# Attention, routing and last stage of a decoder layer: earlier loads of w_out and modulation rows, a smaller first load, and a gated sum on TensorE

## The chip, the cores and the metric

One core of one Trainium2 chip runs the whole program. The metric is device time in microseconds (us), as the median of several runs. The profiler records one execution. Engines are called as in the profile: PE is TensorE (PEld its weight loads), DVE is VectorE, ACT is ScalarE, POOL is GpSimd, SP is SyncE.

## The reference, cut to what matters

A prompt of 2048 tokens and a group of 8 samples with 4 new tokens each (positions from 4096 on, with paged K and V) go through one layer with the same weights, everything in float32:

```python
mod = (silu(c) @ w_ada + b_ada)                      # shift1, scale1, gate1, shift2, scale2, gate2: one row per sequence
proj = (rms_norm(x, norm_mix) * (1 + scale1) + shift1) @ w_in          # q | k | v | xr | yb
# stick-breaking attention, 8 heads of 64:
z = q k^T / 8 + bias;  A[t,s] = sigmoid(z[t,s]) * prod_{s<j<t} (1 - sigmoid(z[t,j]))  for s < t
attn = rms_norm(A v, norm_attn);  rg = rms_norm(rg_lru(conv(xr)) * gelu(yb), norm_rg)
x = x + gate1 * (concat(attn, rg) @ w_out)                              # w_out is 1024 x 1024
xn2 = rms_norm(x, norm_ffn) * (1 + scale2) + shift2
# 32 experts: best group of 4, two best experts e0, e1 in it, with gates g0, g1
ffn = g0 * expert[e0](xn2) + g1 * expert[e1](xn2)
y = rms_norm(x + gate2 * ffn, final_norm)
```

The samples' attention reads 32 pages of 128 keys each, for K and for V, named by a page table: 256 pages of 256 KB each of K and of V.

## The kernel before

The program is a row of phases. Each is a block in which every engine runs its own written-out list of instructions; semaphores order them, and a barrier stands between blocks. There is no planner: the order is that of the Python loops.

**Attention (`attention_phase`, L813).** The prompt's attention goes over 4 pairs of heads and 16 query tiles of 128; 80 items (pair, two query tiles, chunk of 512 keys) of four steps each make 320 steps ("ticks", loop L1348 for PE, L1067 for ACT, L1184 for DVE). In each, PE multiplies q and k (L1244), ACT takes two sigmoids (L1090, L1092), DVE scans (L1208) and multiplies (L1114), PE transposes (L1257) and multiplies by v (L1277). Between them lie 16 units of 19 ticks for the samples. Unit u takes K pages 4 x 4 at a time: `k_turn` (L1290) transposes them out of two buffers `kp` (4 pages each), `sample_scores` (L1300) multiplies them with q, one unit later `sample_values` (L1317) multiplies by the V pages in two buffers `vp`. Each goes with `g = 4 * u + j`.

SP issues in this order (L948 to L973): the page table; `load(0)`, which is q, k and v of the first pair (`qT`, `kT`, `vv`, 1 MB each, L931 to L935); eight small loads of gain and bias (L952, L953), for which DVE waits once at tick 1 (L1211); then for each u and j: wait until group g - 2 has been transposed, four K pages (L921). After group 1 come the new v rows, `load(1)` of the second pair and a wait for the zeros; after j = 1 and j = 3 of each unit `zero_rows` (L937), which writes 1 MB of zeros to the buffers of routing in HBM. `load(2)` and `load(3)` follow units 4 and 8. POOL issues the V pages (L1011), each when its buffer is free. The transposed K lies in `kTs`, which is the memory of `rowsP` and `rowsS`. q, k of the pairs lie in the memory of the first expert's weights.

**Routing (`router_phase`, L1374).** 17 tiles of tokens (the 32 sample tokens first, then 16 of 128). For each tile PE multiplies by the two halves of `w_out` (L1580), DVE multiplies by the modulation row gate1 and adds x (L1645, L1650), then come norm, transposes, logits, the choice of experts and POOL's scatters. At its head SP issues nf_row, the first half of `w_out`, the first rg tile, the second half, x and the router's weights and biases (L1439 to L1461), and POOL the modulation rows `rowsS` and `rowsP` (L1476, L1477). DVE waits for `small` (nf_row and the two biases) and `rows` before its first work (L1720, L1721); PE waits for each half of `w_out` (L1572).

**Experts (`experts_phase`, L1792)** is untouched.

**Last stage (`final_phase`, L1987).** 17 tiles again, with four buffers of two rows per token. POOL gathers the two experts' rows of each token by indirect DMA (L2038); ACT scales the first by its gate (L2048); DVE adds the second times its gate (L2071) and, for even tiles, multiplies by gate2 (L2077); for odd tiles POOL does this (L2029). DVE adds x (L2085). ACT squares, sums and roots (L2053, L2055); DVE takes the reciprocal (L2090) and scales by `final_norm` (L2094); SP stores (L2019). POOL waits for tile i - 3 to be added before it gathers tile i + 1.

## Time and profile before

| | |
|---|---|
| median of 3 runs | 3034.0 us (3031.31 to 3037.3) |
| profiled execution, its own time | 3027.28 us |
| its span, first to last instruction | 3025.3 us |
| attention, about | 728 to 1572 us of the span |
| routing, about | 1573 to 1883 us |
| experts, about | 1884 to 2908 us |
| last stage, about | 2917 us to the end |

Busy time is time in which an engine had an instruction; idle time is put down to what ended it ("<-"). The granted clock is PE's, as a share of 2.4 GHz. A matmul of 512 float32 columns stands as two records that overlap.

### The profile page before, as it was taken

What the parts mean: (1) busy time and instruction counts of PE and PEld (TensorE: products, weight loads), DVE (VectorE), ACT (ScalarE), POOL (GpSimd) and SP (SyncE); (2) the same over time, 40 slices, a digit from 0 to 9 for tenths busy, and PEclk for the clock granted to TensorE, in tenths of its full rate; (3) what the DMA queues carried; (4) which work ended last, traced back from release to release, by engine and by line L of the source; (5) the groups of instructions that cost most, each with busy time, mean ns of one, the idle gap of its engine ahead of it and who ended that gap; (6) DMA issues with size and microseconds to landing.
All of it is one profiled execution on the core that took longest, in us unless ns stands there. A gap on an engine that the chain in (4) does not pass through costs nothing. (4 is left out here: it accounts for less than half of the span.)

```text
span 3025.3 us, 45306 instructions
## 1 busy us (share of the span) xinstructions
PE 2673.0 (88%) x15001; PEld 1337.1 (44%) x15001; DVE 1362.8 (45%) x2735; ACT 973.7 (32%) x1841; POOL 504.4 (17%) x679
## 2 busy tenths in 40 slices
PE   7999999986899898999969999499999998999940
PEld 3444444432444444444434555255555554455520
DVE  2232314132687787887866777222122221122237
ACT  2222222212677676777751212111001010001024
POOL 0101010101011111112110222211111111111136
PEclk9999999997899999999999999699999999999975
DMA  8020201028566667667645433676986579868737
GB/s 313 14 84 14 84 14 56 14 83 322 172 234 232 232 225 239 218 214 252 203 158 162 140 126 132 217 247 213 308 279 210 196 240 362 289 230 278 243 118 248
DMA packets 275673, 575.74 MB, mean 190 GB/s; under 512 B 59278, under 2 KB 75727, under 8 KB 271236
## 3 DMA queue, kind: packets, MB, share of 16 engines
q1 hardware_dynamic: 192464, 425.37, 40.5%
q0 software_dynamic: 82704, 148.06, 15.5%
q8 instruction: 89, 1.46, 0.2%
q14 instruction: 92, 0.75, 0.1%
q10 hardware_dynamic: 324, 0.10, 0.0%
HBM read 460.86 MB, written 112.29 MB: 189 GB/s over the span
## 5 line engine op out<-in xcount | busy, mean ns | idle before, releaser
L1921 PE MATMUL h<-w,xT 128*64 128x256 f32 x5120 | 588.4, 383 | 21.7 <-DMA w<-in_w 17.2
L1921 PEld LDWEIGHTS h<-w,xT 128*64 128x64 f32 x5120 | 362.6, 138 | 242.9 <-issue 73.5
L1208 DVE TENSOR_TENSOR_SCAN left<-leave,left 128x512 f32<-128x512 f32 (+3 forms) x320 | 358.6, 1121 | 162.9 <-ACT leave L1090 161.7
L418 PE MATMUL bank<-xnT,w_in 128*128 128x512 f32 x768 | 330.3, 592 | 0.0
L1934 PE MATMUL yb<-w,hT 128*64 128x512 f32 x1280 | 307.0, 600 | 0.0
L1902 ACT ACTIVATE sg<-h 128x128 f32<-128x128 f32 x160 | 44.4, 278 | 688.5 <-PE h L1921 688.5
L1011 POOL DMA_DIRECT2D vp<-in_cache_v x256 | 137.8, 538 | 690.1 <-issue 685.1
L1580 PE MATMUL pb<-w_out,featT 128*128 128x512 f32 x512 | 227.7, 597 | 1.0 <-DVE t L1645 1.0
L418 PEld LDWEIGHTS bank<-xnT,w_in 128*128 128x128 f32 x768 | 145.6, 190 | 181.8 <-issue 180.3
L1967 DVE TENSOR_TENSOR sg<-sg,h 128x128 f32<-128x128 f32 x160 | 46.1, 288 | 387.5 <-ACT sg L1902 387.5
L418 PE MATMUL bank<-w_in,xnT 128*128 128x512 f32 x512 | 220.4, 592 | 0.0
L1090 ACT ACTIVATE leave<-zb,nbiasP 128x512 f32<-128x512 f32 (+3 forms) x320 | 203.8, 637 | 8.6 <-PE zb L1250 8.6
L1092 ACT ACTIVATE take<-zb,biasP 128x512 f32<-128x512 f32 (+3 forms) x320 | 206.4, 645 | 0.0
L1257 PE MATMUL tb<-ident,take 128*128 128x128 f32 x1088 | 187.7, 289 | 20.6 <-DVE take L1114 16.0
L1114 DVE TENSOR_TENSOR take<-take,left 128x512 f32<-128x512 f32 (+3 forms) x320 | 194.8, 609 | 15.8 <-DVE left L1208 0.4
L1244 PE MATMUL zb<-w 64*128 64x512 f32 (+3 forms) x640 | 166.1, 597 | 31.3 <-ACT take L1092 19.1
L1257 PEld LDWEIGHTS tb<-ident,take 128*128 128x128 f32 x1088 | 116.7, 142 | 165.7 <-issue 106.2
L1290 PE MATMUL tb<-ident,kp 128*128 128x128 f32 x1024 | 160.3, 280 | 30.3 <-DMA kp<-in_cache_k 16.8
L1277 PE MATMUL ob<-wT,vv 128*64 128x256 f32 (+1 forms) x1152 | 183.4, 398 | 1.7 <-ACT wT L1022 1.6
L1022 ACT ACTIVATE wT<-tb 128x512 f32<-128x512 f32 (+3 forms) x240 | 131.0, 546 | 100.7 <-PE tb L1257 99.9
L1876 POOL DMA_DIRECT2D ys_d<-y x82 | 69.2, 844 | 509.1 <-DMA ys_d<-y 443.8
L418 PEld LDWEIGHTS bank<-w_in,xnT 128*128 128x128 f32 x512 | 97.3, 190 | 122.5 <-issue 122.5
(373 smaller groups left out, 2841.6 us busy)
## 6 DMA issues: line engine op xcount, KB each, us to landing
w<-in_w SPq DMA_DIRECT2D x96, 2048.0 KB, 23.5
vp<-in_cache_v POOLq DMA_DIRECT2D x256, 256.0 KB
kp<-in_cache_k SPq DMA_DIRECT2D x256, 256.0 KB
ys_d<-zeros SPq DMA_DIRECT2D x32, 816.0 KB
slab<-in_w_ada SPq DMA_DIRECT2D x24, 1024.0 KB, 13.4
ys_d<-y POOLq DMA_DIRECT2D x83, 256.0 KB, 9.9
x_in<-xs_d POOLq DMA_DIRECT2D x162, 128.0 KB, 6.3
w_in<-in_w_in SPq DMA_DIRECT2D x5, 2048.0 KB, 20.6
```

Source lines behind the costliest of these rows:

```text
L418: mm = pe.matmul(ps[:, :], w, m, start=(i == 0), stop=(i == len(parts) - 1))
L1090: act.activation(leave[n % 4][:, 0:cols], zb[n % 3][:, 0:cols], ACT.Sigmoid, scale=-SCALE, bias=keep["nbiasP"][:, head:head + 1]).then_inc ...
L1092: act.activation(take[n % 4][:, 0:cols], zb[n % 3][:, 0:cols], ACT.Sigmoid, scale=SCALE, bias=keep["biasP"][:, head:head + 1]).then_inc(s_ ...
L1114: dve.tensor_tensor(take[n % 4][:, 0:cols], take[n % 4][:, 0:cols], left[n % 4][:, 1:cols + 1], ALU.mult).then_inc(s_w, 1)
L1208: dve.tensor_tensor_scan(left[n % 4][:, 0:cols][:, ::-1], leave[n % 4][:, 0:cols][:, ::-1], leave[n % 4][:, 0:cols][:, ::-1], left[n % 4][ ...
L1244: mm = pe.matmul(zb[(n + par) % 3][:, 0:cols], qT[pair % 2][half, t * P:t * P + P], kT[pair % 2][half, c * GRP:c * GRP + cols], start=True ...
L1257: mm = pe.transpose(to[:, j * P:j * P + P], take[n % 4][:, j * P:j * P + P], ident[:, :])
L1277: mm = pe.matmul(o[64 * par:64 * par + 64, q0:2 * P], vv[pair % 2][:, c * TPG + j, 64 * par:64 * par + 64], wT[m % 2][par][:, j, :, :].rea ...
L1290: mm = pe.transpose(to[:, i * P:i * P + P], kp[g % 2][:, i, f * P:f * P + P], ident[:, :])
L1580: mm = pe.matmul(pb[half][0:n, :], lhs, w_out[:, c, half * 512:half * 512 + 512], start=(c == 0), stop=(c == KC - 1))
L1921: mm = pe.matmul(h[half][q * G:q * G + G, 0:2 * P], xT[:, c % (XW // P), c // (XW // P) * G:c // (XW // P) * G + G], w13[i][:, c, :, cols] ...
L1934: mm = pe.matmul(yb[p * G:p * G + G, :], hT[:, half, q * G:q * G + G], w2[i][:, q * (EC // STRIPS) + half, p * XW:p * XW + XW], start=(hal ...
```

## The change

- **Attention, start.** The first 512 columns of q and k of pair 0 are loaded first with a semaphore of their own, before the page table; the rest follows. PE waits for the first at item 0 and for the rest at item 2. `load(1)` moves from after group 1 to after unit 1. The zero rows of unit 0's j = 1 go, and each later one moves back by one place; the last stands behind all K pages.
- **Attention, end.** `kp` and `vp` now lie in the memory of `w_out`, which is kept over attention and routing, in the layout (half, chunk, 512). SP loads the first half of `w_out` when the last K group is transposed, then both modulation rows when the last sample scores are done, and the second half when the last sample values are done. The loads of the same name leave the head of routing, from SP and from POOL.
- **Last stage.** Six gather buffers instead of four. ACT makes two diagonal matrices of the gates per tile out of the identity; PE multiplies them with the two gathered row sets and sums them in PSUM (four sets of two banks). DVE multiplies the sum by gate2 (reading PSUM) for every tile. POOL only gathers.

```diff
@@ attention_phase
-        kp = [k.sb(f"kp{i}", [P, PPC, WA]) for i in range(2)]
-        vp = [k.sb(f"vp{i}", [P, 4, WA]) for i in range(2)]
+        kp = [keep["w_out"][:, 0, PPC * i:PPC * i + PPC, :] for i in range(2)]
+        vp = [keep["w_out"][:, 1, PPC * i:PPC * i + PPC, :] for i in range(2)]
...
-                def load(pair):
+                def load(pair, start=0):
...
-                    sp.dma_start(qT[i], io["qT_d"][rows, :]).then_inc(s_kq[i], 16)
-                    sp.dma_start(kT[i], io["kT_d"][rows, :]).then_inc(s_kq[i], 16)
+                    sp.dma_start(qT[i][:, start:], io["qT_d"][rows, start:]).then_inc(s_kq[i], 16)
+                    sp.dma_start(kT[i][:, start:], io["kT_d"][rows, start:]).then_inc(s_kq[i], 16)
...
+                sp.dma_start(qT[0][:, 0:GRP], io["qT_d"][0:P, 0:GRP]).then_inc(s_kq0, 16)
+                sp.dma_start(kT[0][:, 0:GRP], io["kT_d"][0:P, 0:GRP]).then_inc(s_kq0, 16)
                 sp.dma_start(pages[:, :], io["page_table"].rearrange("(a b) n -> a (b n)", a=1)).then_inc(s_pg, 16)
-                load(0)
+                load(0, GRP)
...
                         if g == 1:
                             new_rows(0)
-                            load(1)
                             sp.wait_ge(s_set, 1)
-                        if j == 1:
+                        if j == 1 and u:
+                            zero_rows(2 * u - 1)
+                        if j == 3:
                             zero_rows(2 * u)
-                        if j == 3:
-                            zero_rows(2 * u + 1)
+                            if u == 1:
+                                load(1)
                             if u == 2:
                                 new_rows(1)
                             if u in (4, 8):
                                 load(u // 4 + 1)
+                zero_rows(2 * NU - 1)
+                w_out_d = io["w_out"][0].rearrange("(c p) n -> p c n", p=P)
+                turned(sp, "k_turn", NU - 1, 4 * FC - 1)
+                sp.dma_start(keep["w_out"][:, 0, :, :], w_out_d[:, :, 0:512]).then_inc(sems["w_out0"], 16)
+                turned(sp, "scores", NU - 1)
+                sp.dma_start(keep["rowsS"][:, :, :], io["mod_d"][1:, :]...).then_inc(sems["rows"], 16)
+                sp.dma_start(keep["rowsP"][:, :, :], io["mod_d"][0:1, :]...).then_inc(sems["rows"], 16)
+                sp.wait_ge(s_spv, PPC * NU)
+                sp.dma_start(keep["w_out"][:, 1, :, :], w_out_d[:, :, 512:1024]).then_inc(sems["w_out1"], 16)
                 sp.wait_ge(s_fill, 48 * NE)
...
-                    if m % PPI == 0 and tile == 0:
+                    if m == 0 and tile == 0:
+                        pe.wait_ge(s_kq0, 32)
+                    elif (m == 2 if pair == 0 else m % PPI == 0) and tile == 0:
                         pe.wait_ge(s_kq[pair % 2], 32 * (pair // 2) + 32)
@@ router_phase
-        w_out = k.sb("w_out", [P, KC, D])
+        w_out = keep["w_out"]
...
-                sp.dma_start(w_out[:, :, 0:512], w_out_d[:, :, 0:512]).then_inc(s["w0"], 16)
...
-                sp.dma_start(w_out[:, :, 512:1024], w_out_d[:, :, 512:1024]).then_inc(s["w1"], 16)
...
-                pool.dma_start(keep["rowsS"][:, :, :], io["mod_d"][1:, :]...).then_inc(s["rows"], 16)
-                pool.dma_start(keep["rowsP"][:, :, :], io["mod_d"][0:1, :]...).then_inc(s["rows"], 16)
...
-                        pe.wait_ge(s[f"w{half}"], 16)
+                        pe.wait_ge(sems[f"w_out{half}"], 16)
...
-                        mm = pe.matmul(pb[half][0:n, :], lhs, w_out[:, c, half * 512:half * 512 + 512], ...)
+                        mm = pe.matmul(pb[half][0:n, :], lhs, w_out[:, half, c, :], ...)
@@ final_phase, POOL
                 for i in range(NTL):
-                    n = size[i]
-                    if i >= SETS:
-                        gated(i - SETS)
-                    if i >= SETS:
-                        pool.wait_ge(s["x2"], i - SETS + 1)
+                    n, b = size[i], i % YS
+                    if i >= YS:
+                        pool.wait_ge(s["mm"], i - YS + 1)
...
@@ final_phase, ACT (first)
-                    act.wait_ge(s_y[b], 32 * (i // SETS) + 32)
-                    act.activation(yy[b][0:n, 0, :], yy[b][0:n, 0, :], ACT.Copy, scale=gates[0:n, 0, i:i + 1]).then_inc(s["g0"], 1)
+                    if i >= SETS:
+                        act.wait_ge(s["mm"], i - SETS + 1)
+                    for j in range(2):
+                        last = act.activation(diag[b][0:n, j, 0:n], keep["ident"][0:n, 0:n], ACT.Copy, scale=gates[0:n, j, i:i + 1])
+                    last.then_inc(s["dg"], 1)
...
@@ final_phase, PE (new)
+                for i in range(NTL):
+                    n, b = size[i], i % SETS
+                    pe.wait_ge(s["dg"], i + 1)
+                    pe.wait_ge(s_y[i % YS], 32 * (i // YS) + 32)
+                    if i >= SETS:
+                        pe.wait_ge(s["x2"], i - SETS + 1)
+                    for half in range(2):
+                        cols = slice(512 * half, 512 * half + 512)
+                        for j in range(2):
+                            mm = pe.matmul(both[b][0:n, cols], diag[b][0:n, j, 0:n], yy[i % YS][0:n, j, cols], start=(j == 0), stop=(j == 1))
+                    mm.then_inc(s["mm"], 1)
@@ final_phase, DVE (summed and added in one)
+                    dve.wait_ge(s["mm"], i + 1)
+                    if i >= SETS:
+                        dve.wait_ge(s_st[b], 16 * (i // SETS))
+                    dve.tensor_tensor(out[b][0:n, :], both[b][0:n, :], rows[n][0:n, 3, :], ALU.mult)
+                    dve.drain()
                     dve.wait_ge(sems["x1_s" if i == 0 else ...], 16)
+                    dve.tensor_tensor(x1[i][0:n, :], x1[i][0:n, :], out[b][0:n, :], ALU.add).then_inc(s["x2"], 1)
...
                 summed(0)
-                added(0)
-                summed(1)
                 for i in range(NTL):
-                    if i + 2 < NTL:
-                        summed(i + 2)
                     if i + 1 < NTL:
-                        added(i + 1)
+                        summed(i + 1)
                     normed(i)
```

## Rows read from the trace of the kernel before

**Rows 1.** Part 1 of the page: busy us, share of the span, instructions.

```profile
PE 2673.0 (88%) x15001; PEld 1337.1 (44%) x15001; DVE 1362.8 (45%) x2735; ACT 973.7 (32%) x1841; POOL 504.4 (17%) x679
```

**Rows 2.** Timeline at the start of attention: start, us, engine, line, work [idle before].

```profile
735.64 0.80 PE L1244 MATMUL zb<-w 64*128 64x128 f32 x4 [11.51 <-DMA w<-kT_d]
...
745.30 0.15 DVE L1213 TENSOR_SCALAR s_nbias<-s_bias 128x1 f32<-128x1 f32 x1 [6.92 <-DMA s_bias<-in_sb_bias]
...
751.83 8.71 SPq L939 DMA_DIRECT2D xs_d<-zeros  x2
...
754.78 0.60 PE L1290 MATMUL tb<-ident,kp 128*128 128x128 f32 x4
...
763.30 11.38 SPq L921 DMA_DIRECT2D kp<-in_cache_k  x8
...
773.54 1.11 PE L1290 MATMUL tb<-ident,kp 128*128 128x128 f32 x4 [8.72 <-DMA kp<-in_cache_k]
```

**Rows 3.** Windows there: busy by engine, granted clock, DMA share, GB/s.

```profile
772.00:782.00 10.00, 8.29 (x42) 4.62 (x44) 4.04 (x6) 5.30 (x11) 0.00 (x0) 0.69 0.62 194
```

**Rows 4.** Timeline of PE: the first sample_scores matmul of units 4, 5, 8, 9, 15.

```profile
988.80 0.62 PE L1300 MATMUL tb<-rowsP,q_blk 128*32 128x512 f32 x2
...
1042.65 0.62 PE L1300 MATMUL tb<-rowsP,q_blk 128*32 128x512 f32 x2
...
1187.65 1.04 PE L1300 MATMUL tb<-rowsP,q_blk 128*32 128x512 f32 x2 [1.58 <-ACT wT L1022]
...
1242.76 0.62 PE L1300 MATMUL tb<-rowsP,q_blk 128*32 128x512 f32 x2
...
1528.71 0.62 PE L1300 MATMUL tb<-rowsP,q_blk 128*32 128x512 f32 x2
```

**Rows 5.** Timeline of the end of attention and the head of routing.

```profile
1565.31 1.06 PE L1317 MATMUL s_ob<-vp,s_wT 128*32 128x512 f32 x8
...
1572.69 0.63 ACT L1517 ACTIVATE o_sq<-oT 128x512 f32<-128x512 f32 x1 [2.13 <-PEq L92]
...
1589.28 9.34 PE L1580 MATMUL pb<-w_out,xnT_s 128*32 128x512 f32 x16 [18.07 <-DMA w_out<-in_w_out]
...
1599.60 7.05 PE L1580 MATMUL pb<-w_out,xnT_s 128*32 128x512 f32 x16
...
1599.97 1.21 DVE L1723 SCALAR_TENSOR_TENSOR rowsS<-rowsS,nf_row 32x1024 f32<-32x1024 f32 x1 [11.23 <-DMA b_r<-in_b_router]
...
1607.70 7.11 PE L1580 MATMUL pb<-w_out,featT 128*128 128x512 f32 x16 [1.05 <-DVE t L1645]
```

**Rows 6.** Windows there.

```profile
1530.00:1540.00 10.00, 8.46 (x58) 2.95 (x50) 5.55 (x9) 6.87 (x12) 0.00 (x0) 1.00 0.00 1
1570.00:1580.00 10.00, 0.30 (x1) 0.11 (x1) 0.88 (x4) 1.20 (x3) 2.09 (x13) 0.67 0.61 212
```

**Rows 7.** Timeline of the last stage: its first ACT, two POOL products ten tiles apart, its last DVE.

```profile
2922.89 1.15 ACT L2048 ACTIVATE w<-w,gates 32x1024 f32<-32x1024 f32 x1 [19.44 <-DMA w<-ys_d,ydest_u]
...
2945.55 2.61 POOL L2029 TENSOR_TENSOR w<-w,rowsP 128x1024 f32<-128x1024 f32 x1
...
3001.30 2.61 POOL L2029 TENSOR_TENSOR w<-w,rowsP 128x1024 f32<-128x1024 f32 x1
...
3020.47 1.28 DVE L2094 SCALAR_TENSOR_TENSOR w<-w,ssq,f_row 128x1024 f32<-128x1024 f32 x1
```

**Rows 8.** The tile view of the last stage: ns min/median/max, first and last start.

```profile
L2038 POOL DMA_INDIRECT w<-ys_d,ydest_u x34: 897/1132/2042, 2918.7 to 3000.3; - x34
L2071 DVE SCALAR_TENSOR_TENSOR w<-w,gates x17: 1267/1278/3650, 2924.2 to 3012.1; 128x1024 f32<-128x1024 f32 x16, 32x1024 f32<-32x1024 f32 x1
L2085 DVE TENSOR_TENSOR w<-w,w x17: 1204/1220/1226, 2926.8 to 3017.4; 128x1024 f32<-128x1024 f32 x16, 32x1024 f32<-32x1024 f32 x1
L2053 ACT ACTIVATE junk<-w x17: 1039/1057/1058, 2931.9 to 3018.7; 128x1024 bf16<-128x1024 f32 x16, 32x1024 bf16<-32x1024 f32 x1
L2094 DVE SCALAR_TENSOR_TENSOR w<-w,ssq,f_row x17: 1274/1285/3139, 2938.4 to 3020.5; 128x1024 f32<-128x1024 f32 x16, 32x1024 f32<-32x1024 f32 x1
```

**Rows 9.** The last stage in windows, and what the DMA view of 2916 to 3025 moved.

```profile
2940.00:3004.00 64.00, 0.00 (x0) 0.00 (x0) 49.35 (x52) 27.57 (x44) 50.65 (x30) 0.50 0.82 275
...
DMA packets 7202, 26.10 MB, mean 239 GB/s; under 512 B 832, under 2 KB 832, under 8 KB 7200
```

More of the change, by code:

```diff
@@ L810, in _, with attention_phase @@
                 dve.drain()
-def attention_phase(nc, io, keep):
+def attention_phase(nc, io, keep, sems):
     PAIRS, TPAIRS, PPI = H // 2, NT // 2, 20
@@ L885, in attention_phase @@
             k.sem(f"p4_{n}") for n in ("set", "z", "lv", "tk", "in", "sc", "w", "t", "cd", "ca", "pv", "o", "fill"))
-        s_kq = [k.sem(f"p4_kq{i}") for i in range(2)]
+        s_kq0, s_kq = k.sem("p4_kq_first"), [k.sem(f"p4_kq{i}") for i in range(2)]
         s_v = [k.sem(f"p4_v{i}") for i in range(2)]
@@ L1418, in router_phase @@
         s = {n: k.sem(f"p6_{n}") for n in (
-            "w0", "w1", "wr", "small", "rows", "set", "cons",
+            "wr", "small", "set", "cons",
             "oh", "or", "oT", "fe", "hd", "mm0", "mm1", "ev0", "ev1", "x1", "xs", "xn", "xT", "xe",
@@ L1429, in router_phase @@
         x_src = io["x_prompt"][0].rearrange("(t p) n -> t p n", p=P)
-        w_out_d = io["w_out"][0].rearrange("(c p) n -> p c n", p=P)
         size = [NS] + [P] * NT
@@ L1579, in out_product @@
                             lhs = keep["rgT_new"][:, c - FC, :]
-                        mm = pe.matmul(pb[half][0:n, :], lhs, w_out[:, c, half * 512:half * 512 + 512], start=(c == 0), stop=(c == KC - 1))
+                        mm = pe.matmul(pb[half][0:n, :], lhs, w_out[:, half, c, :], start=(c == 0), stop=(c == KC - 1))
                     mm.then_inc(s[f"mm{half}"], 1)
@@ L1720, in _ @@
                 dve.wait_ge(s["small"], 48)
-                dve.wait_ge(s["rows"], 32)
+                dve.wait_ge(sems["rows"], 32)
                 for n in (NS, P):
@@ L2062, in _ @@
                     squared(i)
+            @block.tensor
+            def _(pe):
+                for i in range(NTL):
[9 more added lines that the diff above has]
+                    mm.then_inc(s["mm"], 1)
             @block.vector
@@ L2140, in build_program @@
         with ExitStack() as inner:
-            keep["oT"] = Kit(nc, inner, clears=False).sb("oT", [P, FC, SEQ])
-            attention_phase(nc, io, keep)
-            router_phase(nc, io, keep)
+            ki = Kit(nc, inner, clears=False)
+            keep["oT"], keep["w_out"] = ki.sb("oT", [P, FC, SEQ]), ki.sb("w_out", [P, 2, KC, 512])
+            for name in ("w_out0", "w_out1", "rows"):
+                sems[name] = k.sem(name)
+            attention_phase(nc, io, keep, sems)
+            router_phase(nc, io, keep, sems)
         with ExitStack() as inner:
```

44 lines of the change are left out of this document (12 added, 32 removed).

## The prediction, made before the change was run

> **What bounds the kernel now.** Part 1 of the page comes first: PE is busy 88% of the span [rows 1]. That is an average, so I went by stage, with windows, and then read the timeline wherever PE was idle. Only three places of the change touch time in which PE does nothing useful. At the start of attention PE sits idle 8.72 us for K pages, and then works at the lower clock [rows 2, 3]. At the head of routing it sits idle 18.07 us for w_out [rows 5]. In the last stage it does nothing at all and its clock stands at 0.50, while DVE, ACT and POOL hand each tile round [rows 7 to 9]. Between these places the order of the work is unchanged, and an earlier start there is an earlier end.
>
> **Part 1, start of attention.** PE's first matmul waits until 735.64 for k [rows 2]. With 256 KB of q and of k in front instead of 1 MB each, it would start some 4 us sooner (a quarter of the data, and the span begins this phase at about 728). I give this nothing: at tick 1 DVE waits for the bias until 745.30, after 6.92 us idle [rows 2], and that load stands behind the same 3 MB of q, k and v as before. Two more issues stand ahead of it, and SP's are a few tenths each, so I charge 0.4 us. Bounds: 1 us lost to 4 gained.
>
> What helps is load(1) and the first zero rows leaving their place. SP was held 8.71 us in the issue of the zeros (behind 3 MB of load(1)), and so issued the K pages of group 2 at 763.30, though the group 0 that frees their buffer was transposed at 755.4 [rows 2]. Now these pages go out at about 757 (some 1.7 us behind the release, as 763.30 stands behind the 761.5 at which SP had finished), four in 3 to 4 us, and land by about 764. PE asked for them at 764.8 (773.54 less 8.72). So the 8.72 us go, with at most 1 or 2 left. The clock goes with them: from 772 to 782 it was granted at 0.69, which is half speed for 6.2 of the 10 us, so PE, which restarted at 773.54, ran some 4.7 us at half speed and lost 2.3 [rows 3]. Together 11.0 us, bounds 6 and 12.
>
> load(1) comes back after unit 1, at j = 3, where load(2) and load(3) stand in units 4 and 8, ahead of the next unit's pages. What such a load costs can be read directly: from unit 4's scores to unit 5's it is 53.85 us, from 8's to 9's 55.11, and from 9's to 15's 285.95 / 6 = 47.66 [rows 4]. The extra is 6.2 and 7.4; I take 6.8. Bounds 4 and 9. The other zero rows keep one per two groups, so they are worth nothing; the last two stand together behind the last pages, and the DMA engines then lie idle (share 0.00 at 1530 to 1540 [rows 6]).
>
> Sum of part 1: -0.4 + 11.0 - 6.8 = +3.8 us gained. Bounds: 7 lost, 9 gained.
>
> **Part 2, end of attention and head of routing.** The first half of w_out (2 MB) and the rows (2.5 MB) go out at about 1526 and 1532, into DMA engines that are idle, 40 us ahead of need: they cost nothing. If that cover were missing they would delay the last V pages. The second half goes out when the last sample values end, at 1566.4 [rows 5], and at the 275 / 0.82 = 335 GB/s that full DMA engines give [rows 9] lands after 6.3 us and some latency, at about 1575. Its first user is PE's second product, not before 1580. SP's last wait, for the zeros, is long met, so the block still ends with DVE.
>
> Routing starts at 1572.7 [rows 5]. Before, PE began its products at 1589.28 and reached the next tile's at 1607.70, 18.4 us later, of which 1.05 were a wait for DVE. It now begins at 1572.8, so this tile is reached at 1572.8 + 17.4 = 1590.2; if the clock is still high, 2.3 us earlier (the first eight products took 9.34 us against 7.05 at full clock). The clock: 0.67 over 1570 to 1580 is full speed until about 1573.4 [rows 6], just after the new start, so it may hold. DVE is the other leg: it starts at 1599.97, when the router's bias lands, and frees PE at 1607.70, 7.7 us later. That bias was issued at the end of SP's queue, behind 4 MB of w_out, and POOL's 2.5 MB shared the engines. Left ahead of it are the rest of the second half, 0.5 MB of nf_row, 0.25 MB of rg, 0.13 MB of x and the router's weights, in many small pieces. 0.9 MB at 335 GB/s is 2.7 us behind 1575, and the small pieces I put at 4 us: about 1581.5, bounds 1579.5 and 1588. DVE then frees PE at 1589.2. I take 1590: gain 1607.7 - 1590 = 17.7 us. Bounds 11.5 (bias at 1588) and 20. The rest of routing runs PE nearly full, so the gain stays.
>
> **Part 3, last stage.** Before, 10 tiles took 3001.30 - 2945.55 = 55.75 us, 5.58 each [rows 7]; the chain is POOL's gathers, its 2.61 us product, DVE's add, and POOL again, since four buffers tie the gather to the add. The product leaves POOL and the buffers are six, so this loop is cut. What is late next, per tile:
> - DVE: two tensor_tensor and one scaling, whose starts lie 1.2 us or so apart (1220 and 1285 ns each [rows 8]), and a reciprocal: 3.95 us. A product that reads PSUM I price as the nearest, 1.22.
> - PE: four products of 512 columns. Eight took 7.05 us at full clock [rows 5], so 3.5; at half clock twice that, 6.9.
> - POOL: two gathers, 1132 ns in the median and up to 2042 [rows 8], with 0.3 between: 2.9, at most 4.7.
> - ACT: two small copies, square, root: about 2.3 by a square of 1.06 [rows 8].
> - DMA: 26.10 MB at 335 GB/s is 78 us for the stage [rows 9], 4.6 a tile.
>
> DVE's account: PE starts tile 0 at 2922.9 [rows 7], at the low clock, 6 us; then 17 x 3.95 = 67.2 us, to 2996.1; the last DVE work ended at 3021.8, 3.5 us before the span's end, so 2999.6: 25.7 gained. DMA's account: from about 2921, 78 less 3 for the last two stores, the last gather lands at 2996; then PE 3.5, DVE 2.5, ACT 1.6, DVE 1.4 and 3.5: 3008.5, 17 gained. They are close enough to disturb each other; I take 21. Bounds 8 and 28.
>
> The shared port is weighed here. A DVE scaling took 3650 ns instead of 1278 where POOL's product ran beside it, and gathers took 0.90 to 2.04 us, the long ones beside DVE work [rows 8]. The Trainium skill, SBUF — State Buffer (Who interferes with whom), says that a DVE instruction with two SBUF inputs contends with a GpSimd instruction that reads SBUF, not with one that only writes it. By it the gathers would be spared, POOL would need 34 x 1.24 = 42 us and be off the path; by the row's long ones it is the first rival below.
>
> **Sum.** 3.8 + 17.7 + 21 = 42.5 us. Against the profiled execution's own 3027.28 us that is 2984.8. The median of the runs shown is 6.7 us above it; I predict for such a median: 3034.0 - 42.5 = 2991.5, rounded 2991.
>
> **Rivals.**
> 1. Gathers become the bound. For it: every second pair took 2.0 us each [rows 8]. Against it: the other pairs took about 1. At 2.3 us for all 34 the last is issued at 2918.7 + 78 = 2997, lands 7 us later, and 12.5 us of tail give 3016.5: 9 gained instead of 21. Time 3003.
> 2. The early K wait stays while load(1) costs its 6.8, because pages wait for something else than SP. For it: V pages and v of pair 0 share the engines. Against it: SP's own hold of 8.71 us. Time 2991 + 11 = 3002.
> 3. The bias lands late (1588): 6 us less, 2997; together with 2, 3008.
> 4. The other side: PE's clock stays low in the last stage. Place: each tile's four products, 6.9 us, and up to 7.6 with an exposed weight load before each. 17 x 7.6 = 129 us from 2922.9, and 9.2 of tail: 3061.3, 36 lost there. Against the 21.5 gained elsewhere that is 14.5 slower: time 3048. It decides from 6.8 us a tile on. For it: PE was at 0.50 throughout [rows 9] and will wait for gathers. Against it: a PE busy without a break was always granted the full clock within some us (the first products of routing rose within their 9.34 us [rows 5]). The Trainium skill, TensorE: Matmul & The Clock Gate (HAM oscillation — how this bites in real kernels), describes it: loops that wait for DMA between bursts of matmuls fall back to the low clock and start each burst slow.
>
> **How the numbers follow.** Forecast (36 to 50 us gained) 0.70; rival 1 0.12; rival 2 or 3 0.13; rival 4 0.03; 0.02 for a mishap that eats the gain. Measurement of this kernel can tell about 0.2%, 6 us, from no change. Faster 0.94, same 0.02, slower 0.04. The range reaches to rivals 1 to 3 and, below, to all upper bounds but a few us: 2976 to 3006.
>
> **What would show it.** In the changed kernel's timeline: no K wait near 765, and a new one of 5 to 7 us some 10 us after the last of unit 1's scores; the first bias wait of DVE still near 745; routing's first product at its block's start and the second tile 17 to 18 us after; DVE in the last stage near 4 to 4.6 us a tile, PE at 1.00 after the first tiles, POOL waiting. The forecast is wrong if gathers keep POOL busy without a break, if PE's clock stays at 0.50, or if routing waits for anything beyond 1585.

## The result and the profile after

| | before | after |
|---|---|---|
| median (lowest to highest) | 3032.65 us (3030.08 to 3037.3) | 2993.23 us (2989.49 to 2995.77) |
| profiled execution: own time, span | 3027.28, 3025.3 us | 2991.91, 2990.2 us |

The ratio is 0.9867, with a 95% interval of 0.985 to 0.9884: 39.4 us less between the medians. The forecast of 2991 us lies 2.2 us below the median and inside the spread of the runs. What follows reads the three places of the prediction again.

Part 1 of the page after, against [rows 1]: PE is busy 66 us more, by the products of the last stage, and POOL and DVE a little less.

```profile
PE 2739.4 (92%) x15137; PEld 1363.8 (46%) x15137; DVE 1347.6 (45%) x2726; ACT 963.5 (32%) x1858; POOL 471.7 (16%) x669
```

**Start of attention.** The timeline after, against [rows 2] (start, duration, engine, line, work, idle time before it and what ended it):

```profile
731.56 6.45 SPq L954 DMA_DIRECT2D s_gain<-in_norm_attn  x1
...
736.02 0.80 PE L1258 MATMUL zb<-w 64*128 64x128 f32 x4 [10.83 <-DMA w<-kT_d]
...
744.46 8.08 SPq L921 DMA_DIRECT2D w_out<-in_cache_k  x8
...
747.51 0.15 DVE L1225 TENSOR_SCALAR s_nbias<-s_bias 128x1 f32<-128x1 f32 x1 [8.76 <-DMA s_bias<-in_sb_bias]
...
751.38 1.12 PE L1304 MATMUL tb<-ident,w_out 128*128 128x128 f32 x4 [2.50 <-DMA w_out<-in_cache_k]
...
759.18 3.64 SPq L921 DMA_DIRECT2D w_out<-in_cache_k  x4
...
849.24 0.98 PE L1304 MATMUL tb<-ident,w_out 128*128 128x128 f32 x4 [4.34 <-DMA w_out<-in_cache_k]
...
998.86 1.12 PE L1304 MATMUL tb<-ident,w_out 128*128 128x128 f32 x4 [9.46 <-DMA w_out<-in_cache_k]
```

The K pages of group 2 go out at 759.18 and the 8.72 us are gone; from 772 to 782 the granted clock is 1.00, not 0.69 [rows 3]. But the bias lands at 747.51, 2.2 us later than before, and PE's first product comes no sooner in spite of its smaller loads. The moved load costs a new wait of 4.34 us at 849.24.

```profile
772.00:782.00 10.00, 9.05 (x66) 5.56 (x67) 8.97 (x17) 8.99 (x19) 0.00 (x0) 1.00 0.61 193
```

The first sample_scores products of units 4, 5 and 15, against [rows 4]. Unit 4 is 5.1 us earlier than before; of this only 0.3 is left at unit 15, since the waits behind load(2) and load(3), which the change does not move, are longer in this profile (9.46 instead of 6.36 us behind load(2)).

```profile
983.71 0.62 PE L1314 MATMUL tb<-rowsP,q_blk 128*32 128x512 f32 x2
...
1039.83 0.62 PE L1314 MATMUL tb<-rowsP,q_blk 128*32 128x512 f32 x2
...
1528.37 0.62 PE L1314 MATMUL tb<-rowsP,q_blk 128*32 128x512 f32 x2
```

**Head of routing**, against [rows 5, 6]. The first product starts with its block; DVE is released at 1583.62, since SP is held 4.74 us in the issue of the first router bias; the second tile's product comes 16.35 us earlier than before.

```profile
1566.10 0.40 SPq L984 DMA_DIRECT2D w_out<-in_w_out  x1
...
1572.38 8.72 PE L1589 MATMUL pb<-w_out,xnT_s 128*32 128x512 f32 x16 [1.52 <-PEq L92]
...
1574.82 4.74 SPq L1467 DMA_DIRECT2D b_r<-in_b_group  x1
...
1583.62 1.21 DVE L1732 SCALAR_TENSOR_TENSOR rowsS<-rowsS,nf_row 32x1024 f32<-32x1024 f32 x1 [8.65 <-DMA b_r<-in_b_router]
...
1591.35 1.10 PE L1589 MATMUL pb<-w_out,featT 128*128 128x512 f32 x2 [2.20 <-DVE t L1654]
```

```profile
1570.00:1580.00 10.00, 7.92 (x15) 1.95 (x16) 1.41 (x7) 0.85 (x2) 1.50 (x14) 0.83 0.90 234
```

**Last stage.** From the issue of f_row to the end of the span it took 107.4 us and takes 85.9. Its timeline and its tile view, against [rows 7, 8]:

```profile
2904.31 0.36 SPq L2023 DMA_DIRECT2D f_row<-in_final_norm  x1
...
2909.59 25.87 PE L2079 MATMUL both<-w,diag 32*32 32x512 f32 x46 [18.69 <-DMA w<-ys_d,ydest_u]
...
2916.71 1.21 DVE L2091 TENSOR_TENSOR w<-both,rowsS 32x1024 f32<-32x1024 f32 x1 [24.86 <-PE both L2079]
...
2922.63 1.23 DVE L2091 TENSOR_TENSOR w<-both,rowsP 128x1024 f32<-128x1024 f32 x1 [3.42 <-PE both L2079]
...
2985.37 1.28 DVE L2101 SCALAR_TENSOR_TENSOR w<-w,ssq,f_row 128x1024 f32<-128x1024 f32 x1
```

```profile
L2079 PE MATMUL both<-w,diag x136: 592/592/1222, 2909.6 to 2977.2; 128*128 128x512 f32 x128, 32*32 32x512 f32 x8
L2041 POOL DMA_INDIRECT w<-ys_d,ydest_u x34: 883/945/1926, 2905.1 to 2956.2; - x34
...
L2091 DVE TENSOR_TENSOR w<-both,rowsP x16: 1203/1218/1225, 2922.6 to 2981.0; 128x1024 f32<-128x1024 f32 x16
```

In windows (busy us of PE, PEld, DVE, ACT, POOL, then granted clock, DMA share, GB/s), against [rows 9]: PE runs its first tiles at 0.50 and rises between 2920 and 2924. From then on DVE is busy 3.6 to 3.85 of 4 us. The DMA engines move 410 to 422 GB/s from 2920 to 2928 and again from 2940 to 2964, which I had not thought they could; between the two it is 340.

```profile
2916.00:2920.00 4.00, 4.00 (x5) 1.51 (x5) 2.42 (x2) 0.76 (x1) 3.08 (x4) 0.50 1.00 395
2920.00:2924.00 4.00, 4.00 (x9) 1.81 (x8) 1.23 (x1) 2.55 (x6) 2.86 (x4) 0.84 1.02 413
2924.00:2928.00 4.00, 4.00 (x10) 1.71 (x9) 3.58 (x4) 2.03 (x5) 2.44 (x2) 1.00 1.02 410
2944.00:2948.00 4.00, 3.82 (x9) 1.44 (x8) 3.85 (x5) 2.03 (x5) 2.29 (x3) 1.00 1.03 422
```

### The profile page after: what moved, and what is told of

Read it like the earlier page. It is cut to its first block and busy times, and to the rows that moved or that the text cites. A ratio compares the mean times of both kernels' runs of the same rounds, so it can differ in the third digit from the quotient of the medians.

```text
span 2990.2 us, 45603 instructions
## 1 busy us (share of the span) xinstructions
PE 2739.4 (92%) x15137; PEld 1363.8 (46%) x15137; DVE 1347.6 (45%) x2726; ACT 963.5 (32%) x1858; POOL 471.7 (16%) x669
## 5 line engine op out<-in xcount | busy, mean ns | idle before, releaser
L1023 POOL DMA_DIRECT2D w_out<-in_cache_v x256 | 137.4, 537 | 689.2 <-issue 687.6
L1258 PE MATMUL zb<-w 64*128 64x512 f32 (+3 forms) x640 | 164.4, 591 | 30.3 <-ACT take L1104 18.7
L1304 PE MATMUL tb<-ident,w_out 128*128 128x128 f32 x1024 | 159.9, 280 | 31.7 <-DMA w_out<-in_cache_k 23.2
```

The source lines that it names most:

```text
L1258: mm = pe.matmul(zb[(n + par) % 3][:, 0:cols], qT[pair % 2][half, t * P:t * P + P], kT[pair % 2][half, c * GRP:c * GRP + cols], start=True ...
L1304: mm = pe.transpose(to[:, i * P:i * P + P], kp[g % 2][:, i, f * P:f * P + P], ident[:, :])
```

## The experiments

All start from the changed kernel. The table reads each profile by stage, in us. The first four columns count from SP's first issue in attention: the end of DVE's bias wait, the first transposed K page, the first product with the samples' q in unit 0, and the first sample_scores product of unit 15. "To tile 2" is from there to the second routing tile's product. "Experts" is from DVE's first fill of `y` there (1916.75 us before) to the issue of f_row, and "last" from that issue to the end of the span. The ratio is to the kernel before, run beside it.

| kernel | bias | first K | unit 0 | unit 15 | to tile 2 | experts | last | median, ratio (95%) |
|---|---|---|---|---|---|---|---|---|
| before | 17.5 | 20.6 | 64.5 | 800.9 | 79.0 | 1001.2 | 107.4 | 3032.7 |
| after | 18.6 | 22.5 | 55.4 | 799.5 | 63.0 | 1003.8 | 85.9 | 2993.2, 0.9867 (0.985 to 0.9884) |
| e10, after again | 18.7 | 22.5 | 55.4 | 795.7 | 63.1 | 1012.1 | 85.4 | 2993.2, 0.9863 (0.9844 to 0.9882) |
| e1, old last stage | 18.7 | 22.6 | 55.3 | 794.7 | 63.0 | 1012.1 | 106.8 | 3013.8, 0.9922 (0.9904 to 0.9939) |
| e2, load(1) early | 18.7 | 22.4 | 65.0 | 801.0 | 63.2 | 1010.3 | 86.9 | 3000.6, 0.9893 (0.9875 to 0.991) |
| e3, whole first loads | 17.5 | 20.7 | 53.1 | 792.9 | 63.1 | 1002.3 | 85.5 | 2988.7, 0.9849 (0.9833 to 0.9866) |
| e4, w_out loaded late | 18.7 | 22.7 | 55.2 | 796.7 | 80.1 | 1003.2 | 85.6 | 3010.2, 0.9921 (0.9898 to 0.9944) |
| e5, four buffers | 18.6 | 22.5 | 55.1 | 791.8 | 63.2 | 1003.7 | 86.6 | 2987.3, 0.9845 (0.9814 to 0.9877) |
| e6, bias by ACT | 11.7 | 22.8 | 55.9 | 797.6 | 62.8 | 1013.9 | 85.9 | 2997.0, 0.9867 (0.9835 to 0.99) |
| e7, loads in parts | 18.6 | 22.6 | 55.5 | 786.3 | 62.7 | 1010.0 | 86.4 | 2983.1, 0.982 (0.9787 to 0.9852) |
| e8, warm PE; bias first | 18.6 | 22.6 | 55.4 | 793.4 | 60.7 | 1009.0 | 83.3 | 2986.0, 0.984 (0.9803 to 0.9877) |
| e11, start order | 10.0 | 12.8 | 44.4 | 782.2 | 62.6 | 1012.5 | 85.5 | 2979.8, 0.9824 (0.9804 to 0.9845) |
| e12, all | 10.5 | 13.4 | 45.6 | 774.8 | 60.7 | 1009.1 | 85.8 | 2970.4, 0.9793 (0.9777 to 0.9808) |

Two columns give the noise. The experts' code is the same in all rows and takes 1001 to 1014 us; the waits for x_in behind it differ from run to run of one kernel (41.8 us in 9 waits after, 48.8 in 13 in e10). And six kernels (after, e10, e1, e4, e5, e8) have the same attention up to unit 15, and reach it at 791.8 to 799.5 us, mean 795.3. The kernel before gave medians of 3033 to 3036 us beside the experiments. But e5's median lies 5.9 us below that of the changed kernel, though its last stage is no shorter. So medians tell some 6 us and more, and the stages must be read for anything smaller.

The spread at unit 15 has a place. From one unit's first sample_scores product to the next, the six agree within 0.3 us up to unit 1 (107.8 to 108.1 us after SP's first issue), and most of what they differ by lies in the three stretches behind a load: unit 1 to 2 (49.7 to 51.4 us), 4 to 5 (53.1 to 56.1) and 8 to 9 (54.4 to 56.1). So an edit at the start is read best at unit 1 or 2. Before, these were at 118.4 and 165.1 us; in the six, unit 2 is at 157.5 to 159.4, mean 158.6.

**e1: the last stage as it was** (all of `final_phase`).

```diff
-                            mm = pe.matmul(both[b][0:n, cols], diag[b][0:n, j, 0:n], yy[i % YS][0:n, j, cols], start=(j == 0), stop=(j == 1))
+                    act.activation(yy[b][0:n, 0, :], yy[b][0:n, 0, :], ACT.Copy, scale=gates[0:n, 0, i:i + 1]).then_inc(s["g0"], 1)
...
```

> The changed kernel with the last stage as it was (GpSimd and VectorE do the gated sum, four gather buffers); everything else as changed. Theory: the stage's 21.5 us (107.4 before, 85.9 after, from the issue of f_row to the end of the span) come from its own work, whatever lies ahead of it: 2993.2 + 21.5 = 3014.7 us, and the stage is again 107 to 108 us long. Rival: part of the 21.5 is a gift of what was changed ahead (the stage begins with other queues and another clock): the stage stays under 102 us and the time under 3009 us.

The stage is 106.8 us again, 20.9 more than after and 21.4 more than in e10; the median is 20.6 us higher. Its gain is its own.

**e2: load(1) and the zero rows at their old places.**

```diff
                             new_rows(0)
+                            load(1)
...
-                            if u == 1:
-                                load(1)
```

> The changed kernel with load(1) and the zero rows back at their old places (load(1) in unit 0 behind the second K page, zero rows at j of 1 and 3); small first loads kept. Theory: the K page stall returns in unit 0 (8.7 us, with some low clock behind it), and the 4.6 us that unit 1 to 2 pays for load(1) go; the later loads cost 3.3 us more after the change than before it, and if that hangs on the order of the zero rows they go too. In sum within 2 us of the changed kernel if the later loads' cost goes (2993 to 2995 us), 4 to 6 us slower if it stays (2997 to 2999 us). Rival: what left unit 0 (8 us and 2.2 of the bias wait) is all gain and unit 1 would have paid its 4.6 us anyway: 8 to 10 us slower, 3001 to 3003 us.

The stall is back, behind the same hold of SP in the zeros' issue as in [rows 2]:

```profile
753.37 8.17 SPq L939 DMA_DIRECT2D xs_d<-zeros  x2
...
764.06 10.71 SPq L921 DMA_DIRECT2D w_out<-in_cache_k  x8
...
774.45 1.11 PE L1302 MATMUL tb<-ident,w_out 128*128 128x128 f32 x4 [8.79 <-DMA w_out<-in_cache_k]
```

Unit 0 is 9.6 us later. From unit 1 to unit 2 it takes 46.7 us, against 49.7 to 51.4 (mean 50.6) in the six kernels above: 3.9 come back. Unit 15 is 5.7 us behind their mean, the median 7.4 us behind. At unit 2, ahead of the loads that scatter, it is 6.9 behind (165.5 against 158.6). That lies between the 4 to 6 us of my theory's second branch and the rival's 8 to 10. The rival's reason falls, since unit 1 to 2 does get its time back. The wait behind load(2) is 8.16 us here, within the 6.85 to 9.46 of the six: it does not hang on where load(1) stands, so the 3 us more of the first profile are within the spread.

**e3: whole first loads.**

```diff
-                sp.dma_start(qT[0][:, 0:GRP], io["qT_d"][0:P, 0:GRP]).then_inc(s_kq0, 16)
-                sp.dma_start(kT[0][:, 0:GRP], io["kT_d"][0:P, 0:GRP]).then_inc(s_kq0, 16)
...
-                load(0, GRP)
+                load(0)
```

> The changed kernel with its first loads whole again (page table, then q and k of pair 0 whole, no small pieces ahead); the moves of load(1), w_out and the rows kept. Theory: the small pieces buy nothing, since TensorE's first product came no earlier with them (736.02 against 735.64 us), and they delay the eight gain and bias loads by 2.2 us: VectorE's bias wait ends near 745.3 instead of 747.5 us and the kernel is 2 us faster, 2991 us. Rival: without the small pieces the first scores come later now, by the time of the longer transfers: the first product at 739 us or later, and the kernel 1 to 4 us slower.

```profile
737.22 0.80 PE L1254 MATMUL zb<-w 64*128 64x128 f32 x4 [11.55 <-DMA w<-kT_d]
...
746.92 0.15 DVE L1223 TENSOR_SCALAR s_nbias<-s_bias 128x1 f32<-128x1 f32 x1 [6.96 <-DMA s_bias<-in_sb_bias]
```

SP's first issue is at 729.39 here, so the first product stands 7.8 us behind it, against 7.1 after: the small loads bring 0.7 us there. The bias comes 1.1 us sooner without them, the first K page 1.8, and unit 0 2.3. Unit 1 keeps it: 105.6 us, against 107.8 to 108.1 in the six. Unit 15 (792.9) is inside their spread, and a median 4.5 us lower is within the noise. The small first loads cost some 2.4 us; the theory holds.

**e4: w_out and the rows loaded in routing again.**

```diff
-                sp.dma_start(keep["w_out"][:, 0, :, :], w_out_d[:, :, 0:512]).then_inc(sems["w_out0"], 16)
...
+                sp.dma_start(keep["w_out"][:, 0, :, :], w_out_d[:, :, 0:512]).then_inc(sems["w_out0"], 16)
+                load_rg(1)
+                sp.dma_start(keep["w_out"][:, 1, :, :], w_out_d[:, :, 512:1024]).then_inc(sems["w_out1"], 16)
...
+                pool.dma_start(keep["rowsP"][:, :, :], io["mod_d"][0:1, :].to_broadcast([P, 4 * D])).then_inc(sems["rows"], 16)
```

> The changed kernel with w_out and the modulation rows loaded again in the head of the routing block, on the queues and at the places they had; their memory stays where the change puts it. Theory: the 16.35 us of the routing head return: first product near 1589, second tile's product some 16.3 us later than after the change, 3009.6 us. Rival: the early loads also cost something at the end of attention or in the experts (2.7 us longer after the change than before), which is got back: 3006 to 3008 us, experts 1001.2 us instead of 1003.8. Second rival: most of the 16 us were TensorE's clock, which fell either way: under 3003 us.

```profile
1587.27 8.55 PE L1586 MATMUL pb<-w_out,xnT_s 128*32 128x512 f32 x16 [18.49 <-DMA w_out<-in_w_out]
```

The wait is back and tile 2 is 17.1 us later; the median is 17.0 higher. Unit 15 (796.7) and the experts (1003.2) stay within their spread, so the early loads cost nothing elsewhere: the theory holds, both rivals fall.

**e5: four gather buffers.**

```diff
-    SETS, YS = 4, 6
+    SETS, YS = 4, 4
```

> The changed kernel with four gather buffers in the last stage instead of six. Theory: in the steady part VectorE sets the pace (3.85 of 4 us busy, 3.87 us a tile), and a gather pair lands some 5 to 6 us after GpSimd issues it, well inside the 11.6 us that three tiles leave it: the stage stays within 2 us of 85.9 us and the kernel within 2 us of the changed one. Rival: with the DMA engines at 410 to 420 GB/s in this stage the gathers need the lead that six buffers give: products wait for gathers, 4.3 to 4.6 us a tile, and the stage is 5 to 10 us longer.

The stage takes 86.6 us against 85.4 to 85.9. POOL waits for products longer (16.7 us in 13 waits, 8.9 in 10 after) and nothing waits for POOL; the median (2987.3) is not higher. The kernels with six buffers and the same stage take 85.4 to 86.9 us, so no gain from the two added buffers is seen.

**e6: gain and bias loads by ACT.**

```diff
-                    sp.dma_start(bias[at, :], io["sb_bias"][0].unsqueeze(1).unsqueeze(2).to_broadcast([H, TS, 1])).then_inc(s_small, 16)
+                    act.dma_start(bias[at, :], io["sb_bias"][0].unsqueeze(1).unsqueeze(2).to_broadcast([H, TS, 1])).then_inc(s_small, 16)
```

> The changed kernel with the eight gain and bias loads at the start of attention issued by ScalarE on its own queue instead of SyncE's, all else as changed. Theory: SyncE's queue, held for 6.5 us at the first of them behind q, k and v, is what makes the bias late and the K pages after it: VectorE's bias wait ends at 740 to 742 us after a start at 728.9 instead of 747.5, SyncE issues the first K page near 735 instead of 744.5, and the scores of unit 0 come 5 to 8 us earlier, the kernel 5 to 8 us faster than the changed one. Rival: the transfers themselves are late, whichever queue issues them (the 16 DMA engines are full with q, k and v): the bias lands at the same time and the gain is under 1.5 us. Second rival: ScalarE's own issues are held as SyncE's were, its first takes come late, and the kernel is no faster or slower.

```profile
735.37 11.43 SPq L921 DMA_DIRECT2D w_out<-in_cache_k  x8
...
751.71 1.12 PE L1304 MATMUL tb<-ident,w_out 128*128 128x128 f32 x4 [9.79 <-DMA w_out<-in_cache_k]
```

```profile
742.00:744.00 2.00, 0.00 (x0) 0.00 (x0) 1.69 (x7) 0.24 (x1) 0.80 (x2) 0.50 1.04 374
744.00:746.00 2.00, 0.00 (x0) 0.00 (x0) 0.00 (x0) 0.00 (x0) 0.54 (x1) 0.50 1.04 384
746.00:748.00 2.00, 0.00 (x0) 0.00 (x0) 0.00 (x0) 0.00 (x0) 0.00 (x0) 0.50 1.02 382
```

My theory fell, and not to either rival as put. The bias came 7 us sooner and SP issued the K pages 9 us sooner, but the first page landed when it had before: the DMA engines were full all the while, at 374 to 384 GB/s. What stands ahead of that page is bytes: 3 MB of q, k and v, and V pages that POOL issues from about 736 on. One wait took the place of the other, and nothing was gained.

**e7: loads of pairs 1 to 3 in three parts**, each two page groups apart.

```diff
-                            if u == 1:
-                                load(1)
-                            if u in (4, 8):
-                                load(u // 4 + 1)
+                        piece = {7: (1, 0), 9: (1, 1), 11: (1, 2), 19: (2, 0), 21: (2, 1), 23: (2, 2), 35: (3, 0), 37: (3, 1), 39: (3, 2)}.get(4 * u + j)
+                        if piece:
+                            load(piece[0], 0, piece[1:])
```

> The changed kernel with q, k and v of pairs 1, 2 and 3 issued one at a time, two page groups apart (load(1): q behind the last page group of unit 1, k and v behind the second and the last of unit 2), instead of all three together. Theory: TensorE's waits for a K page after each load (4.3 us near 849, 7 to 9.5 near 998, up to 7 near 1199 us) come of the K pages queued behind 3 MB at once, and a third of it at a time hides in the lead of two page groups: the waits shrink to under 2 us in all and the last scores come 10 to 14 us earlier. Rival: the bytes are the same, the page groups' lead is spent thrice in small pieces, and the sum of the waits stays within 4 us of what it is.

```profile
895.20 1.12 PE L1307 MATMUL tb<-ident,w_out 128*128 128x128 f32 x4 [3.39 <-DMA w_out<-in_cache_k]
...
991.54 0.66 PE L1307 MATMUL tb<-ident,w_out 128*128 128x128 f32 x4 [1.10 <-DMA w_out<-in_cache_k]
```

Unit 15 is 9.0 us ahead of the six kernels' mean and 5.5 ahead of the best of them; the median is 10.1 us lower. That is a little under the 10 to 14 expected, and the gain is not where the theory had it. Between units it stands so, against the six kernels' mean:

| stretch | with the load whole | e7, in parts | e12, in parts |
|---|---|---|---|
| unit 1 to 2, then 2 to 3 (load(1)) | 50.6 + 50.3 | 46.7 + 54.7 | 46.7 + 50.3 |
| unit 4 to 5 (load(2)) | 54.8 | 47.6 | 47.6 |
| unit 8 to 9 (load(3)) | 55.2 | 53.7 | 54.3 |

So load(2) in parts brings 7.2 us. Load(1) in parts brings nothing in e7: its cost moves one unit on (the 3.39 us above), and it brings its 3.9 only in e12. Load(3) brings 1 to 1.5, for most of what is long in its stretch is not a wait for pages at all. PE waits there for a copy by DVE, 4.69 us in e12, where the load is in parts, as in e10, where it is whole:

```profile
1177.28 1.09 PE L1310 MATMUL tb<-ident,w_out 128*128 128x128 f32 x4 [4.69 <-DVE wT L1141]
```

**e8: three products of no use at the head of the last stage, and the router's biases loaded first.**

```diff
+                for i in range(3):
+                    pe.matmul(both[SETS - 1][:, 0:512], keep["ident"][:, :], keep["rowsP"][:, 0, 0:512], start=True, stop=True)
...
                 sp.dma_start(nf_row[:, :], io["norm_ffn"].to_broadcast([P, D])).then_inc(s["small"], 16)
+                sp.dma_start(b_r[:, 0:NG], io["b_group"].to_broadcast([P, NG])).then_inc(s["small"], 16)
+                sp.dma_start(b_r[:, 8:RW], io["b_router"].to_broadcast([P, NE])).then_inc(s["small"], 16)
```

> Two edits of the changed kernel that lie in different stages, read by stage. Last stage: three products of no use on TensorE ahead of the first tile, while the first gathers are under way (0.85 us for each of two halves at the lower clock, 5.1 us in all). Theory: TensorE's clock, granted at 0.50 until 2920.6 us (16.3 us after the stage's start, 11 after its first product), rises some 5 us earlier; tile 1's product is at full clock, and VectorE's 3.4 us wait for it shrinks to under 1 us: stage 2.5 to 3.5 us shorter than 85.9. Rival: the clock rises at the same time: nothing, or the stage is longer by what the three hold the first tile back. Routing: the two router biases are loaded right behind the first load of that block. Theory: VectorE is released near 1581 instead of 1583.6 us, and TensorE's 2.2 us wait before the second tile's product goes, 2 us gained. Rival: the bias lands no earlier, as what holds it is the queue's transfers ahead and not its place.

```profile
1571.06 1.21 DVE L1732 SCALAR_TENSOR_TENSOR rowsS<-rowsS,nf_row 32x1024 f32<-32x1024 f32 x1 [2.86 <-DMA b_r<-in_b_router]
```

```profile
2900.00:2902.00 2.00, 1.56 (x2) 0.84 (x3) 0.00 (x0) 1.59 (x6) 0.80 (x1) 0.50 0.27 88
2902.00:2904.00 2.00, 2.00 (x4) 0.86 (x3) 0.00 (x0) 0.11 (x1) 1.39 (x3) 0.61 0.69 242
2904.00:2906.00 2.00, 1.44 (x4) 0.24 (x3) 0.00 (x0) 0.00 (x0) 1.54 (x2) 1.00 0.55 111
...
2910.00:2912.00 2.00, 1.51 (x2) 0.83 (x3) 1.48 (x2) 0.41 (x1) 1.70 (x2) 0.59 1.03 350
2912.00:2914.00 2.00, 2.00 (x4) 0.76 (x3) 0.00 (x0) 1.94 (x3) 1.39 (x3) 0.55 0.99 369
2914.00:2916.00 2.00, 2.00 (x6) 0.87 (x5) 0.17 (x1) 0.96 (x4) 1.70 (x2) 1.00 1.01 410
```

Routing: DVE is released 5.4 us after PE's first product instead of 11.2, and tile 2 comes 2.3 us sooner, as expected. Last stage: the clock rises some 3 us after the first of the three, so tile 0 runs at full speed and the stage is 2.1 to 2.6 us shorter. But PE then waits 1.55 us for tile 1's gathers, the clock falls again, and DVE's wait for tile 1 does not shrink (4.28 us).

In e12, with the same three products, the stage took 85.8 us. There the clock fell sooner, near 2890.7, in the middle of tile 0 and with PE busy without a break since 2888.24:

```profile
2888.24 4.59 PE L2087 MATMUL both<-w,diag 32*32 32x512 f32 x8 [0.22 <-DMA w<-ys_d,ydest_u]
```

```profile
2886.00:2890.00 4.00, 3.78 (x9) 1.02 (x8) 0.00 (x0) 0.00 (x0) 2.91 (x4) 0.84 0.59 180
2890.00:2894.00 4.00, 3.40 (x6) 0.84 (x5) 1.06 (x1) 0.00 (x0) 2.95 (x4) 0.59 0.94 311
```

So the wait for the gather is not what the fall needs. Whether the three products are worth anything is open.

**e10: the changed kernel again.**

> The changed kernel once more, word for word, as the measure for what differs between profiles of the same code: its stages ahead of any edit ran 791.8 to 799.5 us from the start of attention to the last scores in four kernels, and 1002 to 1014 us in the experts, where nothing differs. Theory: its attention, up to the last scores, falls within that spread and below the 799.5 of its first profile, so that the gain of part 1 is larger than that one profile showed, 4 to 7 us; the time stays near 2993 us. Rival: 799.5 is what this version gives, and the shorter ones come of their edits.

The theory holds: unit 15 at 795.7, not 799.5.

**e11: another order at the start.** ACT issues the small loads as in e6, v of pair 0 goes behind the first K page group, and POOL's first V page behind the second.

```diff
-                load(0, GRP)
+                load(0, GRP, (0, 1))
...
+                        if g == 0:
+                            load(0, 0, (2,))
...
                 pool.wait_ge(s_pg, 16)
+                pool.wait_ge(s_kp[1], 64)
```

> The changed kernel with another order at the start of attention: the gain and bias loads issued by ScalarE; SyncE's order is the small q and k, the page table, the rest of q and k, the first K page group, v of pair 0, the second group; and GpSimd holds its first V pages until the second K group has landed. Theory: what bounds the start is bytes ahead of the first K pages (the 16 DMA engines are full from 734 to 751 us at 310 to 400 GB/s, and with ScalarE's issues alone the K page landed no earlier), so with v (1 MB) and the V pages (2 MB) behind them the first K page is there at 741 to 743 us instead of 751.4, and the scores of unit 0 come 7 to 10 us earlier (45 to 48 us after the start instead of 55), the kernel 7 to 9 us faster than the changed one. Rival: the queue of SyncE is held for other reasons, or v and the V pages are late then (TensorE waits for them near 758 or behind the scores of unit 0), and under 3 us are left.

```profile
734.56 3.68 SPq L921 DMA_DIRECT2D w_out<-in_cache_k  x4
738.28 0.59 SPq L939 DMA_DIRECT2D vv<-out_v_prompt  x1
...
741.09 1.12 PE L1311 MATMUL tb<-ident,w_out 128*128 128x128 f32 x4 [0.46 <-DMA w_out<-in_cache_k]
...
746.54 0.65 PE L1298 MATMUL ob<-wT,vv 128*64 128x256 f32 x4
```

With v and the V pages behind it, the first K page is transposed at 741.09 with 0.46 us of wait, and v is there when it is wanted. Unit 0 is 11.0 us earlier than after, unit 15 13.1 ahead of the mean, the median 13.4 us lower. The theory holds; its size was too small. The edit moves three things at once (the small loads, v, and the V pages), and what each is worth alone was tried only for the small loads: nothing (e6).

**e12: e7, e11 and both edits of e8 together.**

> All that helped or should: the start order of the run before it, the loads of pairs 1 to 3 in three parts, the router biases first, three products ahead of the last stage's first tile. Theory: the gains lie in different stages and add up: start 7 to 9, loads 6 to 9, routing 2.4, last stage 2.6, in sum 18 to 23 us: 2970 to 2975 us where the changed kernel gives 2993. Rival: the start and the loads share one lead of the K pages, and what the first gives is spent at the next load (the last scores come only as early as with the loads in parts alone): 8 to 12 us, 2981 to 2985.

2970.4 us, 22.8 below the changed kernel, the best of all. By stage: unit 15 20.5 ahead of the mean (13.1 and 9.0 would be 22.1), tile 2 2.3, last stage nothing, in sum 22.8. The start and the loads do not share one lead. That the sum meets the median to a tenth is chance, since the untouched experts alone differ by up to 12 us between profiles.

## Why the prediction was right

Term by term, in us gained; measured by stage, with the runs that isolate a term.

| term of the prediction | predicted | measured | from |
|---|---|---|---|
| small first loads, two more issues | -0.4 | -2.4 | unit 1: e3 to the six |
| early K stall and low clock | +11.0 | +11.4 | unit 0: before to e3, 64.5 to 53.1 |
| load(1) behind unit 1 | -6.8 | -3.9 | unit 1 to 2: 46.7 to 50.6 |
| part 1 | +3.8 | +6.5; +5.6 (1.4 in the first profile) | unit 2: 165.1 to 158.6; unit 15: 800.9 to 795.3 |
| part 2 | +17.7 | +16.0; 17.1 | profiles before and after; e4 |
| part 3 | +21 | +21.5; 21.4 | profiles; e1 against e10 |
| sum | 42.5 | 39.4 between medians | |

**Part 1** had the mechanism right and two sizes wrong, which nearly cancel: that is luck. The terms add up to 5.1, and unit 2 shows 6.5. The other 1.3 us lie between units 0 and 1, where the clock dips longer before (0.77 and 0.89 over 800 to 820) than after (0.83 and 1.00 over 792 to 812). E12 has that longer stretch too (51.9 us against 50.7), without the stall, so it is not counted as the stall's.

The small loads were charged with two issues, a few tenths; they delay the bias by 1.1 and the first K page by 1.8 us. What I gave them at nothing (PE's earlier first product) is 0.7 us, hidden as I said. load(1) was priced by the stretches of load(2) and load(3) [rows 4] and cost 3.9, not 6.8. The reading of the second stretch was wrong: with load(3) in parts it is still 53.7 us long (e7), with PE waiting 4.69 us for DVE, so most of its 7.4 us were not the load's. The first was about right (7.2 for 6.2). Rival 2, that the stall stays, fell: e2 brings SP's hold and the stall back together. It moves load(1) and the zero rows at once, so which of the two makes the hold was not tried.

**Part 2**: the step that failed is the landing of the bias, 1583.6 instead of 1581.5, since SP is held 4.74 us in its issue. That is why PE waits 2.20 us for DVE, and e8 gets them back. The clock was not full all through the new start (0.83 over 1570 to 1580), one of the two cases I left open. w_out and the rows cost nothing where they went, as said (e4). Rival 3 fell.

**Part 3**: 21 was a middle between two accounts, and only one of them was true; that it met 21.5 is luck. DVE's account gave 25.7. Its steady term held: 3.87 us a tile for 3.95, the product that reads PSUM 1218 ns for 1220. Its head was too short: tile 0 kept DVE waiting 7.1 us, not 6, and tile 1 another 3.42, because the clock was still at 0.50 for most of its products; 25.7 - 1.1 - 3.4 = 21.2. The DMA account (17) rests on 335 GB/s for full engines, a rate scaled up from the old stage at share 0.82, and the new stage moves 410 to 422 for most of its time. The Trainium skill, DMA: Bandwidth & Descriptors (Specifications), gives 435 GB/s as the ceiling of the fabric; the trace is in line with that, 422 being 97% of it. So rival 1 was never near: POOL waited for PE, and with four buffers as well (e5). The 34 gather issues took 36.2 us in all, against 47.1 before. With 0.3 us between them that is 1.36 each, where the account without disturbance had 1.24; some still took 1.4 to 1.9 us.

Rival 4 was seen only as a start: at 0.50 for 11.7 us after PE's first product, then 1.00 to the end of the products. What spoke against it in the prediction, that a busy PE soon gets the full clock, did not hold for tile 0: PE was busy for its 7.1 us and stayed at 0.50. The Trainium skill's account of clocks that fall in DMA waits (TensorE: Matmul & The Clock Gate, HAM oscillation — how this bites in real kernels) fits e8, where the clock fell after PE had waited 1.55 us for a gather, but not e12, where it fell with no such wait.

**The sum** lies 3 us above the medians' 39.4. The stages measured give 5.6 + 16.0 + 21.5 = 43.1; the rest is within what the untouched experts differ by (1001.2 us in the profile before, 1003.8 and 1012.1 in two of the changed kernel). But 1001.2 is the shortest of all thirteen profiles, and the kernel before has only the one. Whether the change costs the experts some us is open.

**The signs** that the prediction named: no K wait near 765, a new one behind unit 1 (4.34 us, not 5 to 7), PE at 1.00 after the first tiles and POOL waiting came as said. DVE's bias wait ended at 747.5 and not near 745, the second routing tile came 19.0 us after the first product and not 17 to 18, and PE's 2.20 us wait for DVE, up to 1591.35, is a wait beyond 1585, which the prediction had named as a sign against it. All three are the late bias loads, in the two blocks.

## What to carry to other kernels

Where a phase begins with the DMA engines full, count the bytes ahead of each first need and order them by when they are wanted, on every queue that feeds the same engines: moving the small loads to another queue only shifted the wait (e6), and with 3 MB moved behind the first pages as well, 13 us came off (e11). Splitting a first load pays only if its user is what waits last, and several MB at once in a stream of pages can be better sent in parts: 7.2 us for load(2), while load(1) in parts brought nothing in e7 and its whole 3.9 in e12. Before a long stretch is put down to a load, look at what the engine waits for in it: with load(3) most of it was something else. When one profile shows an unchanged stage slower by a few us, run the same kernel again before explaining it.

## What the hardware showed that was not expected

- Full DMA engines do not move one rate: 314 GB/s (share 1.14) from 738 to 740 us after, while the small gain and bias loads run, 374 to 384 (1.02 to 1.04) a little later in e6, 410 to 422 (1.02 to 1.03) in most of the last stage.
- SP is held in an issue while earlier transfers are under way: 6.45 us at the first gain load after, 4.74 at the router's bias, 11.43 for eight K pages in e6. In e6 ACT issued the same eight small loads within 6 us and was not held, but it began at 728.91, together with the loads of q, k and v and not behind them on one queue, so this does not tell whether its queue would be held.
- PE's clock rose 11.7 us after the first product of the last stage after, but 3.1 us after the first of the three added products in e8, and 4.1 in e12. Tile 0 has 32 rows in its weights, the three and every later tile have 128. After, the clock stayed at 0.50 through the 7.1 us of tile 0 and rose 4.7 us into tile 1; in e12 it fell in the middle of tile 0. Whether the 32 rows are the cause was not tried.
